# Five stages whose second token tile is transposed two blocks earlier in TensorE's queue

## The chip, the cores and the metric

The kernel runs on one core of one Trainium2 chip. The metric is the time of one execution on the device in microseconds (us). Beside it there is one execution under the hardware profiler; its rows are what this document reads. PE or TensorE is the matmul engine (PEld its weight loads), DVE is VectorE, ACT is ScalarE, POOL is GpSimd, SP is SyncE, which issues the weight DMAs. A difference of under about 0.3%, 2.9 us here, can't be told from no change.

## What is computed

Two small transformer blocks in float32, one after the other, over 256 tokens of width 1024. The first has a differential-attention and Fourier mixer, two gated feed-forward layers and a convolution module; the second a gated linear recurrence and a block attention. What matters here is what stands ahead of five of the large products: a normalised and modulated copy of the state x is multiplied by a weight matrix.

```python
def rmsnorm(x, g):
    x32 = x.astype(jnp.float32)
    y = x32 * lax.rsqrt(jnp.mean(x32 * x32, axis=-1, keepdims=True) + EPS)
    return (y * g.astype(jnp.float32)).astype(x.dtype)

def modulate(h, shift, scale):
    return h * (1 + scale) + shift

def swiglu(h, w1, w3, w2):
    return (jax.nn.silu(h @ w1) * (h @ w3)) @ w2

def conformer_conv(h, pw1_w, ...):
    a, g = jnp.split(h @ pw1_w + pw1_b, 2, axis=-1)
...
        x = x + mod_l[2] * y_l
        x = x + mod_l[5] * swiglu(modulate(rmsnorm(x, ffn_norm_g[i]), mod_l[3], mod_l[4]),
                                  ffn_w1[i], ffn_w3[i], ffn_w2[i])
```

The five products are h @ w1 and h @ w3 of the two feed-forward layers (stages ffn0 and ffn1), the first product of the convolution module (pw1), the input product of the recurrence (rg_in) and the key and value product of the block attention (kv).

## The kernel before

**Products.** Every float32 operand is split into a high and a low part (`hi`, `lo`), and a product is three matmuls: hi by hi, hi by lo, lo by hi (`three`, L2059 to L2063). Each of the three has a 128x128 piece of the state as stationary operand and 512 columns of a weight unit as moving operand. Three such matmuls are called a block here. The 256 tokens are two tiles of 128 (t = 0, 1), the width 1024 is eight pieces of 128 (k = 0 to 7). A weight unit holds four pieces k by 512 columns, so that a chunk of 512 output columns takes two units: j = 0 with k = 0 to 3 and j = 1 with k = 4 to 7. `half(u, j, ..., ts, ks)` (L2068) issues the blocks of unit u for the tiles ts and, of the unit's four pieces, for those in ks. Results of tile t accumulate in PSUM bank t. Units are loaded by SP into `w_land`, copied by ScalarE to `w_hi` and subtracted by VectorE to `w_lo`; three of each exist. A unit counts as used (`s_used`) with the last block of tile 1.

**The first chunk of a stage.** The operand of these five stages isn't ready when the stage before ends, and it is made tile by tile. For one tile: VectorE and ScalarE finish the residual sum and its squares, VectorE the mean, GpSimd the power -1/2 (`rstd`, L518), VectorE scales the tile (`tile_normed`, L1363, output `xn`, semaphore `xn`), TensorE transposes the eight 128x128 pieces into two PSUM banks (`turn_tile`, L2096 to L2101, semaphore `tr`), VectorE applies scale and shift to pieces 0 to 3 (L1400, `xfull` or `kv_full`), ScalarE to pieces 4 to 7 (L755), ScalarE copies each to `xT_hi` (L766), VectorE subtracts it to `xT_lo` (L1383, semaphore `lo`). Each block of a first chunk waits for its own `lo` (L2076).

VectorE does this in the order of `tile_operand` (L1377): the pieces of tile 0, between them a last residual step and the mean of tile 1, then `tile_normed` of tile 1, then at once the first half of the split of the third weight unit (`split_lo_half`, L1370), then the pieces of tile 1, with the unit's second half ahead of the last three subtractions. ScalarE's order is `tile_hi` (L750).

**TensorE's order** is `first_chunk` (L2103): the transposes of tile 0 (in ffn0, ffn1 and kv they have already been issued inside the last half of the stage before, L2427), four blocks of unit u and four of unit u + 1 for tile 0, the transposes of tile 1, then the eight blocks of tile 1. The blocks are numbered b0 to b15 in this document. Each engine runs its instructions in the order in which they are written, and one that waits holds up those behind it.

The transposes of tile 1 go to banks 2 and 3 (AFTER_DENSE) or 3 and 5 (AFTER_FFN), which nothing else reads at that time; the blocks go to banks 0 and 1.

Callers of `first_chunk` are `ffn` (L2485, twice), `dense` (L2407, for pw1 and kv) and the loop of rg_in (L2650). After the first chunk of ffn0 TensorE also waits for the sums of a modulation job (`job_sum`, L1274 on VectorE, summed at L2141) and for a tile of zeros (L596, GpSimd).

Of the kernel before, what the change touches and what calls it, by code (L numbers as in the profile page):

```python
# [182 lines left out]
def build(nc, t_in, out):  # L183
    with ExitStack() as ctx:
        sems = {}

        def sem(name):
            if name not in sems:
                sems[name] = ctx.enter_context(nc.semaphore(name))
            return sems[name]  # L190

        def seen(kind, stage, n):

            return sem(kind), STEPS_BEFORE[kind, stage] + n
# [4 lines left out]
        def place(name, shape, offset, dtype=F32):  # L199
            return nc.alloc_sbuf_tensor_at(name, shape, dtype, offset=ARENA + offset)  # L200
# [8 lines left out]
        xT_hi = place("xT_hi", [P, KT, S], 164 * KB, R32)  # L209
        xT_lo = place("xT_lo", [P, KT, S], 172 * KB, R32)  # L210
# [144 lines left out]
        bank = [ctx.enter_context(nc.psum_tensor(f"bank{i}", [P, 512], F32)) for i in range(8)]  # L355
# [1702 lines left out]
        def _(pe):  # L2058
            def three(dst, hi, lo, whi, wlo, start, stop):  # L2059

                pe.matmul(dst, hi, whi, start=start, stop=False)  # L2061
                pe.matmul(dst, hi, wlo, start=False, stop=False)  # L2062
                return pe.matmul(dst, lo, whi, start=False, stop=stop)  # L2063

            def unit_wait(u, i=None):
                pe.wait_ge(s_lo, at(u + 1, i, 6))

            def half(u, j, hi, lo, banks, last=None, ready=None, ts=range(NT), ks=range(4), part=False):  # L2068

                wh = w_hi[u % N_SPLIT][:, :].rearrange("p (k n) -> p k n", k=4)  # L2070
                wl = w_lo[u % N_SPLIT][:, :].rearrange("p (k n) -> p k n", k=4)
                for t in ts:
                    for k in ks:

                        if ready is not None and ADDS[ready]["lo"] == NT * KT:
                            pe.wait_ge(*seen("lo", ready, KT * t + 4 * j + k + 1))  # L2076
                        elif ready is not None and t == 0:
                            pe.wait_ge(*seen("lo", ready, min(4 * j + k + 1, ADDS[ready]["lo"])))
                        kt = 4 * j + k
                        ins = three(banks[t][:, :], hi[:, kt, t * P:t * P + P], lo[:, kt, t * P:t * P + P],  # L2080
                                    wh[:, k, :], wl[:, k, :], kt == 0, kt == KT - 1)
                    if part and j == 1 and t == 0:
                        ins.then_inc(sem("part"), 1)
                if last is not None:
                    ins.then_inc(last, 1)
                return ins
# [9 lines left out]
            def turn_tile(stage, t, banks):  # L2096

                pe.wait_ge(*seen("xn", stage, t + 1))
                for k in range(KT):
                    pe.transpose(bank[banks[t][k // 4]][:, P * (k % 4):P * (k % 4) + P],  # L2100
                                 xn[:, t, k * P:k * P + P], ident[:, :]).then_inc(sem("tr"), 1)  # L2101

            def first_chunk(stage, u, banks, turned=False):  # L2103

                if not turned:
                    turn_tile(stage, 0, banks)
                for j in range(2):
                    unit_wait(u + j)
                    half(u + j, j, xT_hi, xT_lo, bank[0:2], None, stage, (0,))
                turn_tile(stage, 1, banks)  # L2110
                for j in range(2):
                    half(u + j, j, xT_hi, xT_lo, bank[0:2], s_used, stage, (1,))

# [132 lines left out]
            for c in (2, 3):  # L2246
                for side, (event, b) in enumerate(events[c]):
# [3 lines left out]
                    for j in range(2):  # L2251
                        u = 2 * c + j
# [141 lines left out]
            def dense(stage, n_chunks, ready=None, after=None, before=None, parts=True, job=(), turn_banks=None,  # L2394
# [4 lines left out]
                for c in range(n_chunks):  # L2399
# [4 lines left out]
                    if c == 0 and first is not None:  # L2404
                        first(u, banks)
                    elif c == 0 and turn_banks is not None:
                        first_chunk(ready, u, turn_banks, turn_banks == AFTER_DENSE)  # L2407
                    elif c == 0 and ready == "ln":
                        for t in range(NT):
# [38 lines left out]
            def ffn(layer, loops, first_job):  # L2448
# [26 lines left out]
                def turn_hidden(c, i=None):  # L2475
# [7 lines left out]
                    ins.then_inc(sem("h_turn"), 1)  # L2483

                first_chunk(f"n_ffn{layer}", base, AFTER_DENSE, True)  # L2485
                if layer == 0:
                    job_sums(first_job - 1)
# [160 lines left out]
            for c in range(4):  # L2648
                if c == 0:
                    first_chunk("n_rg", BASE["rg_in"], AFTER_FFN)  # L2650
                for j in range(2 if c else 0):
                    u = BASE["rg_in"] + 2 * c + j
                    unit_wait(u)
                    for t in range(NT):
                        half(u, j, xT_hi, xT_lo, bank[2 * (c % 2):2 * (c % 2) + 2], s_used if t == 1 else None,
                             None, (t,))
                        if (c, j, t) == (1, 0, 0):
                            turn_pair("rg_in", rg_tok, rg_free)(0)
                        for g in {(2, 0, 1): (2, 3), (2, 1, 0): (4, 5), (2, 1, 1): (6, 7)}.get((c, j, t), ()):
                            rg_gate_mm(g)  # L2660
                    if (c, j) == (1, 1):
                        job_sums(15)
                if c == 3:
                    unit_wait(BASE["rg_out"])
                    half(BASE["rg_out"], 0, xT_hi, xT_lo, bank[0:2], None, "rg", (0,))
                if c >= 1:
                    turn_pair("rg_in", rg_tok, rg_free)(c)
                if c == 1:
                    job_turn(15)
                    pe.wait_ge(s_cols, cols_upto(15))  # L2670
                    rg_gate_mm(0)
                    rg_gate_mm(1)
# [214 lines left out]
```

## Time and profile before

| | |
|---|---|
| timed runs | 973.63, 975.66, 975.75 us, median 975.66 |
| the profiled execution's own time | 974.42 us |
| its span, first to last instruction | 972.8 us |
| mean granted TensorE clock over the span | 0.986 of full |
| busy: TensorE, VectorE, ScalarE, GpSimd | 93%, 76%, 48%, 14% |
| the five first chunks begin about (us) | ffn0 206, pw1 408, ffn1 523, rg_in 727, kv 821 |
| bytes moved | 229 MB, 236 GB/s in the mean |

Times in rows are microseconds from the start of the span. Busy time of TensorE includes the modelled end of each matmul, so a matmul of 0.39 us starts about 0.23 us after the one before it; distances between starts say more than durations. A wait row says which engine and line waited for which, with the total, the number of waits and the longest.

### The profile page before, as it was taken

To read this page: it belongs to the slowest core of one execution; us is meant where nothing else is said; L and a number is where in the kernel's file an instruction comes from. 1 tells how busy PE (TensorE), PEld (TensorE's weight loads), DVE (VectorE), ACT (ScalarE), POOL (GpSimd) and SP (SyncE) were. 2 spreads that over 40 slices of the span, in tenths; PEclk is the share of its full clock that TensorE was granted. 3 is DMA by queue.
4 is the path that set the end of the run, shared out by engine and by line. 5 is a ranking of instruction groups with operands and counts; after the bars stand their busy time and mean duration, and the time that the engine had idled before them with its cause. 6 is when DMAs were issued, how large, how long until landed. Compare 5 with 4: busy or idle time off the path is not lost.

```text
span 972.8 us, 12490 instructions
## 1 busy us (share of the span) xinstructions
PE 906.0 (93%) x4323; PEld 711.8 (73%) x4323; DVE 739.7 (76%) x1075; ACT 468.6 (48%) x782; POOL 134.8 (14%) x204
## 2 busy tenths in 40 slices
PE   3899999989999999899988999999979998999995
PEld 1687666767888888677566788888867776778874
DVE  1598779888768677779678877678698888876675
ACT  2462258554344443553185444434435876545661
POOL 0011130405001300020003210021001110001000
PEclk9999999999999999999999999999989999999998
DMA  9998653459989889457525798898857446695001
GB/s 332 375 356 287 225 174 124 168 175 340 379 304 304 314 288 316 159 172 260 201 87 164 254 354 320 281 332 299 290 172 250 130 165 204 227 358 193 23 23 43
DMA packets 121094, 229.09 MB, mean 236 GB/s; under 512 B 8650, under 2 KB 64684, under 8 KB 121050
## 3 DMA queue, kind: packets, MB, share of 16 engines
q1 hardware_dynamic: 94656, 141.57, 42.4%
q0 software_dynamic: 24224, 86.32, 25.5%
q10 hardware_dynamic: 2170, 0.64, 0.3%
q8 instruction: 24, 0.39, 0.2%
q14 instruction: 20, 0.16, 0.0%
HBM read 227.43 MB, written 1.08 MB: 235 GB/s over the span
## 4 chain that ended last, share of the span: by engine, by line
PE 68%; DVE 16%; issue 6%; ACT 4%; DMA 4%; POOL 1%; SPq 0%; POOLq 0%; ACTq 0%; DVEq 0%
PE bank L2061 19%; PE bank L2063 18%; PE bank L2062 18%; DVE job_sum L1274 2%; DVE w_lo L1257 2%; DMA a_land<-ada_w_dram 2%; PE bank L2640 1%; DMA x<-x_dram 1%; DVE x L1339 1%; DMA w_land<-ev_w_in_dram 1%; ACT w_hi L696 1%; DVE tmp L1338 1%; DVE w_lo L1370 1%; PE bank L2481 1%; PE bank L2293 1%
## 5 line engine op out<-in xcount | busy, mean ns | idle before, releaser
L2061 PE MATMUL bank<-w_hi,xT_hi 128*128 128x512 f32 x800 | 322.9, 404 | 16.9 <-DVE xT_lo L1383 10.0
L2063 PE MATMUL bank<-w_hi,xT_lo 128*128 128x512 f32 x800 | 313.2, 392 | 0.0
L2062 PE MATMUL bank<-w_lo,xT_hi 128*128 128x512 f32 x800 | 312.8, 391 | 0.0
L1257 DVE TENSOR_TENSOR w_lo<-w_land,w_hi 128x2048 fp32r<-128x2048 f32 x109 | 250.1, 2298 | 79.8 <-ACT w_hi L696 79.6
L696 ACT ACTIVATE w_hi<-w_land 128x2048 fp32r<-128x2048 f32 x109 | 208.2, 1915 | 110.9 <-PE bank L2063 102.2
L2061 PEld LDWEIGHTS bank<-w_hi,xT_hi 128*128 128x128 f32 x800 | 151.0, 189 | 61.8 <-issue 19.4
L2063 PEld LDWEIGHTS bank<-w_hi,xT_lo 128*128 128x128 f32 x800 | 150.7, 188 | 32.7
L1274 DVE SCALAR_TENSOR_TENSOR job_sum<-a_land,silu_c,job_sum 128x1024 f32<-128x1024 f32 x126 | 163.4, 1297 | 11.0 <-DMA a_land<-mod_w_dram 4.4
L2062 PEld LDWEIGHTS bank<-w_lo,xT_hi 128*128 128x128 f32 x800 | 151.1, 189 | 28.2
L2061 PE MATMUL bank<-w_hi,hT_hi 128*128 128x512 f32 x176 | 69.9, 397 | 2.8 <-DVE hT_lo L1688 2.8
L2063 PE MATMUL bank<-w_hi,hT_lo 128*128 128x512 f32 x176 | 68.7, 390 | 0.0
L2062 PE MATMUL bank<-w_lo,hT_hi 128*128 128x512 f32 x176 | 68.5, 389 | 0.0
L526 POOL DMA_DIRECT2D a_land<-ada_w_dram x40 | 29.3, 732 | 226.8 <-DVE job_sum L1274 226.8
L989 ACT ACTIVATE silu_g<-bank 128x256 f32<-128x256 f32 x44 | 14.5, 382 | 76.1 <-PE bank L2063 76.1
L993 ACT ACTIVATE hT_hi<-bank 128x512 fp32r<-128x512 f32 x22 | 13.2, 599 | 68.1 <-PE bank L2481 68.1
L2061 PEld LDWEIGHTS bank<-w_hi,hT_hi 128*128 128x128 f32 x176 | 33.0, 188 | 13.8 <-issue 7.3
L2063 PEld LDWEIGHTS bank<-w_hi,hT_lo 128*128 128x128 f32 x176 | 33.0, 188 | 7.1
L2062 PEld LDWEIGHTS bank<-w_lo,hT_hi 128*128 128x128 f32 x176 | 33.1, 188 | 6.5
L526 POOL DMA_DIRECT2D a_land<-mod_w_dram x24 | 17.2, 717 | 146.4 <-DVE job_sum L1274 140.7
L1370 DVE TENSOR_TENSOR w_lo<-w_land,w_hi 128x1024 fp32r<-128x1024 f32 x30 | 36.3, 1218 | 0.4 <-ACT w_hi L742 0.4
L726 ACT ACTIVATE sq_half<-x 128x512 f32<-128x512 f32 x24 | 15.2, 631 | 42.9 <-DVE x L1339 42.9
L1684 DVE TENSOR_TENSOR hid<-silu_g,bank 128x256 f32<-128x256 f32 x44 | 16.5, 417 | 23.4 <-ACT silu_g L989 23.4
(327 smaller groups left out, 1115.0 us busy)
## 6 DMA issues: line engine op xcount, KB each, us to landing
w_land<-ffn_w_dram SPq DMA_DIRECT2D x132, 512.0 KB, 5.8
a_land<-ada_w_dram POOLq DMA_DIRECT2D x40, 1024.0 KB, 6.1
a_land<-mod_w_dram POOLq DMA_DIRECT2D x24, 1024.0 KB, 5.8
w_land<-od_pw_w_dram SPq DMA_DIRECT2D x24, 512.0 KB, 5.2
w_land<-ev_w_in_dram SPq DMA_DIRECT2D x20, 512.0 KB, 11.6
w_land<-ada_w_dram SPq DMA_DIRECT2D x16, 512.0 KB, 10.6
a_land<-kv_mod_w_dram POOLq DMA_DIRECT2D x8, 1024.0 KB, 6.6
w_land<-rg_w_in_dram SPq DMA_DIRECT2D x16, 512.0 KB, 5.2
```

The costliest lines, as they stand in the source:

```text
L526: pool.dma_start(a_land[j % 2][:, :].rearrange("p (k n) -> p k n", k=2), kview(w)[:, 2 * j:2 * j + 2, bass.ds(col, D)]).then_inc(a_landed[ ...
L696: act.activation(w_hi[u % N_SPLIT][:, :], w_land[n % N_LAND][:, :], ACT.Copy).then_inc(s_hi, 1)
L726: act.activation(sq_half[:, n % 2, :], x[:, t, 512 * c:512 * c + 512], ACT.Square, accum_out=ss[:, 2 * t + c:2 * t + c + 1]).then_inc(sem( ...
L989: act.activation(silu_g[:, t, :], bank[t][:, 0:256], ACT.Silu).then_inc(sem("silu_g"), 1)
L993: act.activation(hT_hi[:, :, :].rearrange("p k s -> p (k s)"), bank[6][:, :], ACT.Copy).then_inc(sem("hT_hi"), 1)
L1257: dve.tensor_tensor(w_lo[u % N_SPLIT][:, :], w_land[n % N_LAND][:, :], w_hi[u % N_SPLIT][:, :].bitcast(F32), ALU.subtract).then_inc(s_lo, 1)
L1274: ins = dve.scalar_tensor_tensor(out=job_sum[:, :], in0=w, scalar=silu_c[:, c, n:n + 1], in1=job_sum[:, :], op0=ALU.mult, op1=ALU.add)
L1370: return dve.tensor_tensor(w_lo[u % N_SPLIT][:, cols], w_land[n % N_LAND][:, cols], w_hi[u % N_SPLIT][:, cols].bitcast(F32), ALU.subtract)
L1684: dve.tensor_tensor(hid[:, t, :], silu_g[:, t, :], bank[t][:, 256:512], ALU.mult).then_inc(sem("hid"), 1)
L2061: pe.matmul(dst, hi, whi, start=start, stop=False)
L2062: pe.matmul(dst, hi, wlo, start=False, stop=False)
L2063: return pe.matmul(dst, lo, whi, start=False, stop=stop)
```

## The change

In `first_chunk` the call of `half` for tile 0 issues for j = 0 the pieces 0 to 3 as before, but for j = 1 only pieces 0 and 1. Then tile 1 is transposed, and then the two blocks that were left (pieces 2 and 3 of unit u + 1, b6 and b7) are issued. After that tile 1's blocks run as before. All blocks accumulate into the same banks in the same order of k. `turn_tile` begins with a wait for `xn`, which moves with it. No other engine's program is changed.

```diff
                 for j in range(2):
                     unit_wait(u + j)
-                    half(u + j, j, xT_hi, xT_lo, bank[0:2], None, stage, (0,))
+                    half(u + j, j, xT_hi, xT_lo, bank[0:2], None, stage, (0,), range(4 - 2 * j))
                 turn_tile(stage, 1, banks)
+                half(u + 1, 1, xT_hi, xT_lo, bank[0:2], None, stage, (0,), (2, 3))
                 for j in range(2):
                     half(u + j, j, xT_hi, xT_lo, bank[0:2], s_used, stage, (1,))
```

## Rows read from the trace of the kernel before

**Rows 1.** The page, first part: busy time, share and instructions of each engine.

```profile
PE 906.0 (93%) x4323; PEld 711.8 (73%) x4323; DVE 739.7 (76%) x1075; ACT 468.6 (48%) x782; POOL 134.8 (14%) x204
```

**Rows 2.** Waits, whole span: who waited for whom, total us, times, longest us.

```profile
PE bank L2061 <- DVE xT_lo L1383: 10.0, 19, 1.3
...
PE bank L2100 <- DVE xn L1363: 8.1, 4, 3.6
```

**Rows 3.** Timeline of ffn0: start us, us, engine, line, operation [idle before <-releaser].

```profile
201.68 0.75 DVE L1363 TENSOR_SCALAR xn<-x,rstd 128x1024 f32<-128x1024 f32 x1 [0.69 <-POOL rstd L518]
...
202.49 1.09 PE L2100 MATMUL bank<-ident,xn 128*128 128x128 f32 x8 [1.63 <-DVE xn L1363]
...
203.34 0.47 PE L2061 MATMUL bank<-w_hi,xT_hi 128*128 128x512 f32 x1
...
204.11 0.40 PE L2061 MATMUL bank<-w_hi,xT_hi 128*128 128x512 f32 x1
...
210.33 0.75 DVE L1363 TENSOR_SCALAR xn<-x,rstd 128x1024 f32<-128x1024 f32 x1
...
211.00 1.22 DVE L1370 TENSOR_TENSOR w_lo<-w_land,w_hi 128x1024 fp32r<-128x1024 f32 x1
211.00 0.40 PE L2061 MATMUL bank<-w_hi,xT_hi 128*128 128x512 f32 x1
...
212.39 1.04 PE L2100 MATMUL bank<-ident,xn 128*128 128x128 f32 x8
213.03 0.73 DVE L1400 TENSOR_SCALAR xfull<-bank,a_col,mcol 128x128 f32<-128x128 f32 x2 [0.82 <-PE bank L2100]
...
214.17 0.50 PE L2061 MATMUL bank<-w_hi,xT_hi 128*128 128x512 f32 x1 [0.73 <-DVE xT_lo L1383]
...
214.96 0.39 PE L2061 MATMUL bank<-w_hi,xT_hi 128*128 128x512 f32 x1
...
217.69 0.50 PE L2061 MATMUL bank<-w_hi,xT_hi 128*128 128x512 f32 x1
...
218.49 0.39 PE L2061 MATMUL bank<-w_hi,xT_hi 128*128 128x512 f32 x1
```

**Rows 4.** Timelines of pw1, ffn1, rg_in and kv: scaling of tile 1, and b8.

```profile
412.30 0.75 DVE L1363 TENSOR_SCALAR xn<-x,rstd 128x1024 f32<-128x1024 f32 x1
...
416.13 0.50 PE L2061 MATMUL bank<-w_hi,xT_hi 128*128 128x512 f32 x1 [0.73 <-DVE xT_lo L1383]
...
527.89 0.53 POOL L596 MEMSET zeros<- 128x512 bf16 x1
...
527.98 0.98 DVE L1363 TENSOR_SCALAR xn<-x,rstd 128x1024 f32<-128x1024 f32 x1
...
531.81 0.50 PE L2061 MATMUL bank<-w_hi,xT_hi 128*128 128x512 f32 x1 [0.74 <-DVE xT_lo L1383]
...
733.21 0.75 DVE L1363 TENSOR_SCALAR xn<-x,rstd 128x1024 f32<-128x1024 f32 x1
...
733.60 0.40 PE L2061 MATMUL bank<-w_hi,xT_hi 128*128 128x512 f32 x1
...
736.76 0.50 PE L2061 MATMUL bank<-w_hi,xT_hi 128*128 128x512 f32 x1 [0.73 <-DVE xT_lo L1383]
...
825.67 0.75 DVE L1363 TENSOR_SCALAR xn<-x,rstd 128x1024 f32<-128x1024 f32 x1
...
829.51 0.50 PE L2061 MATMUL bank<-w_hi,xT_hi 128*128 128x512 f32 x1 [0.73 <-DVE xT_lo L1383]
```

**Rows 5.** The chain that ended last, behind ffn0's first chunk: start us, us, what.

```profile
221.58 0.55 POOL zeros L596
```

**Rows 6.** Stretches: length, busy PE, PEld, DVE, ACT, POOL; PEclk, DMA share, GB/s.

```profile
194.40:218.70 24.30, 20.63 (x94) 15.66 (x93) 20.36 (x43) 14.16 (x37) 2.06 (x3) 1.00 0.52 174
...
243.00:267.30 24.30, 24.30 (x116) 19.59 (x116) 19.06 (x15) 9.37 (x9) 2.15 (x3) 1.00 1.05 378
...
724.20:731.00 6.80, 5.98 (x18) 4.74 (x19) 5.71 (x14) 4.35 (x17) 0.00 (x0) 0.50 0.50 154
```

## The prediction

> **What bounds the kernel now.** I read the page's busy shares first: TensorE is busy 906.0 of 972.8 us [rows 1]. Then who waited for whom: on TensorE the waits that touch this change are for the turned operand and for the normalised tile [rows 2]. Then the timeline of one of the five stages, ffn0 [rows 3], the same steps in the other four [rows 4], the chain behind the first [rows 5], and the busy time in slices [rows 6], which tells whether time won early in a stage is still there at its end.
>
> I call three matmuls of 128x512 (the call of `three`) a block. A stage's first chunk has sixteen: b0 to b7 for token tile 0, b8 to b15 for tile 1. The kernel before runs b0 to b7, eight transposes of tile 1, then b8 to b15. Rows 3 show what is wrong with that. The last transposes start at 212.39, VectorE gets its first turned piece at 213.03 (it had sat idle), and b8 starts at 214.17, after TensorE sat idle 0.73 us waiting for `xT_lo`. VectorE's scaling of tile 1 had ended long before, at 210.33 + 0.75 = 211.08. So between two stretches of work lies a dead time: transposes, scale, split, subtract, one after the other with nothing else to run. In rows 4 the four other stages have the same picture.
>
> **The change, part by part.** Nothing is added or removed: the same 48 matmuls and 8 transposes per stage. The transposes and their one wait (for the scaled tile, semaphore `xn`) move ahead of b6 and b7. No DMA is issued by the moved step, and SP's and GpSimd's queues are not passed. Behind the wait on TensorE's queue stand, newly, b6 and b7, which are ready by then; nobody waits for their results until tile 1 is done (the count for a used weight unit goes up only at tile 1's blocks), so delaying them costs nothing on another engine.
>
> The new start T of the transposes is the later of b6's old start and the scaled tile. In ffn0 b6 started at 211.00 and the tile is ready at 211.08. The first turn of the same kind started 0.06 after its scale ended (202.43 to 202.49) [rows 3]. So T = scale's end + 0.06, in ffn0 211.14, a new wait of 0.14. In rg_in it is the longest: 733.21 + 0.75 + 0.06 = 734.02 against b6 at 733.60, so 0.42 [rows 4].
>
> From T: eight transposes take the queue 0.85 (202.49 to 203.34), the block after them 0.77 (203.34 to 204.11) [rows 3]. A block in a running stream takes a little under 0.70; from the distance of b6 to the turn, (212.39 - 211.00) / 2, it is 0.69. So b8 can start at T + 0.85 + 0.77 + 0.69 = T + 2.31, if its operand is there.
>
> Operand side: VectorE runs the half split `w_lo` (1.22) right behind the scale, from 211.00, and can then take the turned piece at about 212.15 instead of 213.03 [rows 3]; the transposes of T = 211.14 give their first four by 211.78 (0.64 from turn to piece, as 212.39 to 213.03). From the piece to b8 it took 214.17 - 213.03 = 1.14, so b8's operand is there at about 213.29; TensorE gets there at 213.45. Both hang on the scale's end, so the margin of some 0.16 is the same in all five stages. The next late thing is TensorE itself, no longer the operand.
>
> Gains at b8, old start less (scale's end + 0.06 + 2.31) [rows 3, 4]:
> ffn0: 214.17 - 213.45 = 0.72
> pw1: 416.13 - (412.30 + 0.75 + 2.37) = 0.71
> ffn1: 531.81 - (527.98 + 0.98 + 2.37) = 0.48
> rg_in: 736.76 - (733.21 + 0.75 + 2.37) = 0.43
> kv: 829.51 - (825.67 + 0.75 + 2.37) = 0.72
> Sum 3.06 us.
>
> In ffn1 the scale took 0.98 where it takes 0.75 elsewhere, and GpSimd's memset of `zeros` runs at that moment (527.89 for 0.53) [rows 4]. In the old order these 0.23 us were hidden, in the new they are on TensorE's path, and they are in the sum. The Trainium skill, page Advanced Engine Details and Errata, section DVE Details, says that one of VectorE's two ports is shared with GpSimd; that is a rule against this change, since it makes TensorE wait for an operation that GpSimd can stretch, and the trace agrees in this one stage.
>
> Second term: a block that starts after a wait takes 0.79 (b8 to b9, 214.17 to 214.96), and so does b13 (217.69 to 218.49), which waited for its operand behind the second half split [rows 3]. In a stream it is 0.69. b8 no longer waits: 5 x 0.10 = 0.50. For b13: its operand came 217.69 - 213.03 = 4.66 after the first piece, now at 212.15 + 4.66 = 216.81; TensorE gets there at 213.45 + 5 x 0.69 = 216.90. That is 0.09 ahead, which may be too little to load weights in advance, so this second restart costs between nothing and what it costs now: a gain of 0 to 0.50, I take the middle, 0.25.
>
> The bound on moving the transposes between b5 and b6 of one accumulation: I know of no row for a turn inside tile 0's own blocks, but the previous dense stage has the same form (202.49 to 204.11 lies inside its last half) and that is the price used. Below nothing it cannot be, since the same eight transposes run anyway; above, the whole 0.85 + 0.08 is already counted.
>
> Sum: 3.06 + 0.50 + 0.25 = 3.8 us, bounds 3.55 and 4.05.
>
> **Does it last to the end?** In ffn0 the old chain behind b15 is not TensorE's but VectorE's: last subtractions, two `job_sum` steps, `zeros` by GpSimd at 221.58, then the next block [rows 5]. VectorE was idle before 213.03 and moves forward by 213.03 - 212.15 = 0.88, so this chain moves as much as the 0.82 to 0.92 that TensorE gains. After it TensorE is busy 24.30 of 24.30 us in the slice from 243, the first of twelve such slices in the two feed-forward loops [rows 6], so time won is kept. In pw1, rg_in and kv what follows waits for the chunk's last matmul or for VectorE, both earlier. I see nothing with its own clock there. All 3.8 us should reach the end.
>
> Against the profiled execution: 974.42 - 3.8 = 970.6. The three timed runs are at 973.63 to 975.75 with a median 1.2 above the profiled one; the mean of all four is 974.87, and I set the forecast from that: 971.1.
>
> **Rivals.**
> (A) Weight supply takes the place of the wait. In the slice from 243 us the DMA share is 1.05, at 378 GB/s [rows 6]: if the stream is the true limit of the feed-forward loops, TensorE, arriving earlier, waits for weights there and the gains of ffn0 and ffn1 (0.9 and 0.6) are lost; what is left is 3.8 - 1.5 = 2.3, so 972.6. Against it: TensorE has no idle in that slice, and the slice is the fullest one. Together with any other loss of one or two stages' gain (972 to 974): 20%.
> (B) The change does nothing: the dead time is VectorE's and ScalarE's own and only moves. It would need VectorE to be late at b8 by itself. The half split after the scale is the candidate; with it I get 213.29 against 214.17, so this cannot hide more than 0.16 of the gain unless the split waits too. Time 974.9. 6%.
> (C) Slower: the scaled tile is late. In the old order it had 212.39 - 211.08 = 1.31 us to spare; now it has less than nothing (0.08 to 0.36 late already). A tile later by d costs TensorE d at once, in each stage, with b6 and b7 stuck behind it although ready. The gain at the end of tile 1 is 0.6 to 0.9 per stage, so the change turns into a loss when the tile comes on average 0.76 us later than in this trace, and a loss of 0.3% needs about 1.35. With 1.35 in each of five stages: 974.9 - 3.8 + 6.75 = 977.8. For it: the stretch of 0.23 in ffn1. Against it: nothing that the scale depends on is changed. 4%.
> (D) Clock. Granted clock was half (1.2 of 2.4 GHz, 0.50 in the row) from 724.2 to 731 us, after TensorE had idled up to 3.6 us waiting for the tile ahead of rg_in [rows 2, 6]. New waits are 0.42 at most, so I expect no new such stretch; but if one of 6.8 us fell into a saturated loop it would lose half of it, 3.4 us: 974.5. The Trainium skill, page TensorE: Matmul & The Clock Gate, section Part 4: PE-mode transpose, says that transposes do not count as busy time for the gate; by that rule eight of them where matmuls ran could bring such a stretch, and the time would be those 974.5. The row speaks against it for this pattern: the granted clock is 1.00 in the slice from 194 to 219, with both turns of ffn0 in it. 5%.
> (E) More than I count: the removal of idle time keeps a stretch at full clock that was at half, or the runs fall low; 968 to 969.5. 5%.
>
> **How the numbers follow.** Forecast 60%, A 20%, B 6%, C 4%, D 5%, E 5%. A measurement of this kernel can tell about 0.3%, 2.9 us, from no change. Faster by more than that: the forecast, E, and a part of A: 0.69. Within: most of A, B, D and the low edge of the forecast: 0.26. Slower: C and the tail of D: 0.05. The range: the forecast with its bounds and the spread of executions (about 1 us either way) is 969.8 to 972.4; A and part of D reach to 974.5. From 969.0 to 974.6 leaves out B, C, most of E.
>
> **What would show it.** In the profile of the changed kernel, in each of five stages: transposes of tile 1 between the sixth and seventh block, starting 0.06 after the scale; b8 2.3 us after them with no wait for `xT_lo`; VectorE idle before the turned piece of tile 1 gone (it was 0.8); TensorE's total wait for `xT_lo` down from 10.0 by about 3.6 and a new wait for `xn` of 0.1 to 0.4 five times, 1.2 in all. The half split of unit 2 and the last subtractions come 0.6 to 0.9 earlier. If b8 still waits, step "operand side" is wrong; if b8 is early and the span is not, the step "does it last" is; the point where the two timelines' difference shrinks will say which rival it is.

## The result, and the profile after

The changed kernel takes 970.59 us (median of its executions beside 975.80 of the kernel before, six each). The ratio is 0.9922 with an interval of 0.9896 to 0.9949. One execution of the changed kernel took 2325.56 us and is left out as a slow one; why isn't known, and the other five lie from 968.63 to 971.68. Forecast was 971.1, range 969.0 to 974.6; carried to the 975.66 given before, the ratio makes 968.05, below the range. So the change gained, at first sight, 7.6 us where the sum says 3.8. The two medians by themselves differ by 5.2 us only. The ratio stands for a kernel before at 970.59 / 0.9922 = 978.2 us; of its six executions three are the ones on record ahead of the prediction (median 975.66), and the other three are 975.84, 978.41 and 979.68 (median 978.41), so the ratio looks like one to these three. A second comparison, with more executions (below), gave 0.995 with 0.9932 to 0.9968, some 4.9 us. What follows has two questions: is the sum of 3.8 right, and where does the rest come from?

The profiled execution took 970.08 us, with a span of 968.4 against 972.8 before. First the page of the changed kernel: span, busy time and the granted clock in slices (the share of full speed that TensorE was given, in tenths).

```profile
span 968.4 us, 12490 instructions
...
PE 906.3 (94%) x4323; PEld 713.0 (74%) x4323; DVE 740.0 (76%) x1075; ACT 468.5 (48%) x782; POOL 136.9 (14%) x204
...
PEclk9999999999999999989999999999989999999998
```

TensorE has the same busy time and count as in [rows 1]; what went is idle time. The waits over the whole span, who waited for whom (total us, times, longest):

```profile
PE bank L2100 <- DVE xn L1363: 8.0, 6, 3.6
...
PE bank L2061 <- DVE xT_lo L1383: 6.5, 14, 1.3
```

Against [rows 2] the wait for `xT_lo` has five cases and 3.5 us less, and the wait for `xn` two cases more. The timeline of ffn0 shows the mechanism (start us, us, engine, line, operation):

```profile
199.39 0.75 DVE L1363 TENSOR_SCALAR xn<-x,rstd 128x1024 f32<-128x1024 f32 x1 [0.69 <-POOL rstd L518]
...
208.04 0.75 DVE L1363 TENSOR_SCALAR xn<-x,rstd 128x1024 f32<-128x1024 f32 x1
208.71 1.22 DVE L1370 TENSOR_TENSOR w_lo<-w_land,w_hi 128x1024 fp32r<-128x1024 f32 x1
208.85 1.09 PE L2100 MATMUL bank<-ident,xn 128*128 128x128 f32 x8
209.69 0.48 PE L2061 MATMUL bank<-w_hi,xT_hi 128*128 128x512 f32 x1
209.84 0.73 DVE L1400 TENSOR_SCALAR xfull<-bank,a_col,mcol 128x128 f32<-128x128 f32 x2
211.18 0.40 PE L2061 MATMUL bank<-w_hi,xT_hi 128*128 128x512 f32 x1
...
214.62 0.39 PE L2061 MATMUL bank<-w_hi,xT_hi 128*128 128x512 f32 x1
...
216.01 0.39 PE L2061 MATMUL bank<-w_hi,xT_hi 128*128 128x512 f32 x1
```

The tile is scaled at 208.04 + 0.75 = 208.79, the turn starts 0.06 later at 208.85, b8 at 211.18 (2.33 after the turn) with no wait, b13 at 214.62 with none, b15 at 216.01. VectorE takes the turned piece right behind the half split, without the idle 0.82 of [rows 3]. Everything ahead of the scaling is untouched by the change, so I measure in each stage from the start of tile 0's scaling (here 199.39; before 201.68, [rows 3]). The last block of the kernel before:

```profile
219.19 0.39 PE L2061 MATMUL bank<-w_hi,xT_hi 128*128 128x512 f32 x1
```

b15 went from 219.19 - 201.68 = 17.51 to 216.01 - 199.39 = 16.62 (rows are rounded, so such a difference is good to 0.02). The other four stages, pw1, ffn1, rg_in and kv, of the changed kernel: the scaling of tile 1, then b8.

```profile
409.10 0.75 DVE L1363 TENSOR_SCALAR xn<-x,rstd 128x1024 f32<-128x1024 f32 x1
...
412.24 0.40 PE L2061 MATMUL bank<-w_hi,xT_hi 128*128 128x512 f32 x1
...
525.64 0.98 DVE L1363 TENSOR_SCALAR xn<-x,rstd 128x1024 f32<-128x1024 f32 x1
...
529.00 0.40 PE L2061 MATMUL bank<-w_hi,xT_hi 128*128 128x512 f32 x1
...
730.35 0.76 DVE L1363 TENSOR_SCALAR xn<-x,rstd 128x1024 f32<-128x1024 f32 x1
...
733.48 0.40 PE L2061 MATMUL bank<-w_hi,xT_hi 128*128 128x512 f32 x1
...
822.22 0.75 DVE L1363 TENSOR_SCALAR xn<-x,rstd 128x1024 f32<-128x1024 f32 x1
...
825.35 0.40 PE L2061 MATMUL bank<-w_hi,xT_hi 128*128 128x512 f32 x1
```

None of these b8 waits, where all of [rows 4] waited 0.73 or 0.74. The table is the ruler for all that follows: the start of b15 after the start of tile 0's scaling, in us, read the same way from each kernel's timeline. The gain is the sum of the five differences to the first line. The kernels whose names begin with e_ are the experiments of the next section.

| kernel | ffn0 | pw1 | ffn1 | rg_in | kv | gain |
|---|---|---|---|---|---|---|
| before | 17.50 | 16.54 | 17.49 | 17.96 | 17.51 | |
| before, again (e_none) | 17.50 | 16.55 | 17.51 | 17.97 | 17.51 | -0.04 |
| the change | 16.62 | 15.64 | 16.79 | 17.38 | 16.59 | 3.98 |
| the change, again (e_two) | 16.58 | 15.66 | 16.80 | 17.37 | 16.58 | 4.01 |
| e_one | 16.81 | 15.88 | 16.82 | 17.36 | 16.79 | 3.34 |
| e_three | 17.23 | (17.28) | 17.44 | 17.98 | 17.21 | 0.60 |
| e_late_old | 17.76 | 16.82 | 17.78 | 18.05 | 17.76 | -1.17 |
| e_late_new | 18.01 | 17.07 | 18.01 | 18.30 | 18.01 | -2.40 |
| e_split3 | 15.74 | (16.01) | 15.92 | 17.39 | 15.71 | 5.70 |
| e_split5 | 15.71 | 15.48 | 16.03 | 17.60 | 15.71 | 6.47 |
| e_memset | 16.59 | 15.65 | 16.60 | 17.36 | 16.60 | 4.20 |
| e_split3m | 15.73 | 15.64 | 15.71 | 17.35 | 15.70 | 6.87 |

A value in brackets fell into a stretch at half clock and isn't in the sum. In rg_in every kernel has such a stretch, before and after the change alike, over some 7 us from the start of tile 0's scaling and done before b5; these values are kept. (In e_three the sum of the other four stands against 3.08 for the change in the same four. In e_split3, whose pw1 is the changed kernel's own, that stage's 0.90 comes to it: 6.6.) The two executions of one kernel, twice, agree within 0.05 in every stage on this ruler; their spans don't.

### The profile page after: what moved, and what is told of

Read it like the earlier page. It is cut to its first block, busy times and chain, and to the rows that moved or that the text cites. A ratio compares the mean times of both kernels' runs of the same rounds, so it can differ in the third digit from the quotient of the medians.

```text
span 968.4 us, 12490 instructions
## 1 busy us (share of the span) xinstructions
PE 906.3 (94%) x4323; PEld 713.0 (74%) x4323; DVE 740.0 (76%) x1075; ACT 468.5 (48%) x782; POOL 136.9 (14%) x204
## 4 chain that ended last, share of the span: by engine, by line
PE 67%; DVE 16%; issue 6%; ACT 5%; DMA 4%; POOL 1%; SPq 0%; POOLq 0%; ACTq 0%; DVEq 0%
PE bank L2061 19%; PE bank L2063 18%; PE bank L2062 18%; DVE job_sum L1274 2%; DVE w_lo L1257 2%; PE bank L2641 1%; DMA a_land<-ada_w_dram 1%; DMA x<-x_dram 1%; DVE x L1339 1%; DVE w_lo L1370 1%; DMA w_land<-ev_w_in_dram 1%; ACT w_hi L696 1%; DVE tmp L1338 1%; PE bank L2482 1%; PE bank L2142 1%
```

## The experiments

Time is judged in two ways: by the ratio to the kernel before, run beside it, and by the ruler. Beside them stands a third figure, the clock-free one. It is an estimate from 161 timed executions: 72 of the kernel before, in three comparisons, and 89 of the nine kernels timed beside it more than once. A straight line of the time against the mean granted clock of each execution is laid through them, with a constant for each kernel. It says 0.54 us (0.07 either way) more for each 0.001 of mean clock less, and for each kernel a difference to the one before that is free of the clock's share. Its 95% interval stands behind it in brackets.

**The comparison itself.** The kernel before against itself, and the changed kernel again, beside 32 executions of the kernel before (median 977.53, from 973.94 to 980.91).

> The kernel before, unchanged, timed against itself. Theory 1 (the change is worth 3.8 us by the order of the queue alone, and what the first comparison showed beyond that, some 7.6 us, is the draw of stretches at half clock): ratio 1.000, but single runs spread over 5 us or more, and the profile shows the half-clock stretches at other places than the first profile of before did, with VectorE's timeline moving by 1 to 3 us at each. Theory 2 (the change itself avoids stretches at half clock): single runs of before all share the same stretches, so they agree within 2 us.

> The changed kernel, two blocks ahead, once more. Theory 1: ratio about 0.996 (3.8 of 975), and wherever the profile's timeline jumps other than in the five first chunks there is a stretch at half clock in one of the two profiles. In the five chunks VectorE's timeline moves forward by 0.9, 0.9, 0.55, 0.6 and 0.9 us. Theory 2: ratio again about 0.992.

Measured: e_none 976.59, ratio 0.9997 (0.998 to 1.0015). e_two 972.81, ratio 0.995 (0.9932 to 0.9968). With the clock taken out: -0.1 (0.8 either way) and -4.0 (0.9 either way). Mean clock of the executions 0.9795 for the kernel before, 0.9813 for e_two, 0.9809 for e_none: the change has no more clock than the kernel before has against itself. So the change is worth about 4 us here, and the reading that it also avoids half-clock time finds no support. The single executions of e_none spread over 4.6 us, where that reading wanted 2. What the spans do instead shows in one row: ffn0's first scaling, ahead of which no instruction differs. First e_none, then e_two:

```profile
199.41 0.75 DVE L1363 TENSOR_SCALAR xn<-x,rstd 128x1024 f32<-128x1024 f32 x1 [0.69 <-POOL rstd L518]
```

```profile
205.07 0.75 DVE L1363 TENSOR_SCALAR xn<-x,rstd 128x1024 f32<-128x1024 f32 x1 [0.69 <-POOL rstd L518]
```

From 199.4 to 205.1: 5.7 us apart in work that is the same. The kernel before had 201.68, the changed one 199.39. The clock is part of it. Stretches of e_two ahead of that row (length, busy PE, PEld, DVE, ACT, POOL, then granted clock, DMA share, GB/s):

```profile
20.00:26.90 6.90, 3.65 (x16) 3.27 (x16) 4.32 (x10) 3.16 (x6) 0.71 (x1) 0.51 1.09 352
43.90:47.30 3.40, 3.40 (x10) 2.63 (x9) 3.26 (x12) 2.03 (x5) 0.00 (x0) 0.50 1.06 385
119.00:125.80 6.80, 6.40 (x25) 4.44 (x25) 2.77 (x6) 0.58 (x2) 1.44 (x2) 0.50 0.69 246
```

That is 17.1 us at 1.2 GHz; e_none has only the first of them, 6.9. The 10.2 us more go with 5.7 us more time; by the line above they would cost 2.8 (10.2 us at half clock are 0.0052 of the mean), so about half of it is not explained. The Trainium skill, page TensorE: Matmul & The Clock Gate, section Part 1: The HAM clock gate, says of a kernel's start that the number of matmuls at the low clock varies from run to run of one kernel. The rows agree in kind, and show such stretches at 43.9 and 119 us as well, far from the start.

**How far ahead.** One block and three blocks instead of two.

```diff
-half(u + j, j, xT_hi, xT_lo, bank[0:2], None, stage, (0,), range(4 - 2 * j))
+half(u + j, j, xT_hi, xT_lo, bank[0:2], None, stage, (0,), range(4 - j))
-half(u + 1, 1, xT_hi, xT_lo, bank[0:2], None, stage, (0,), (2, 3))
+half(u + 1, 1, xT_hi, xT_lo, bank[0:2], None, stage, (0,), (3,))
```

(for three: `range(4 - 3 * j)` and `(1, 2, 3)`)

> Tile 1 turned one block ahead (b7 alone behind the turn). By the sum: the transposes start at b7's old start, after the scaled tile is ready, so no new wait; the operand is then the last thing at b8 in ffn0, pw1 and kv. b8 comes earlier than before by 0.69, 0.68, 0.66, 0.60, 0.68 = 3.3 us, and b8 still pays the 0.10 of a restart. Gain at the stages' ends about 3.3 to 3.6, so 0.2 to 0.5 less than two blocks ahead; in ffn1 and rg_in a little more than two ahead at b8. The rival, that waiting for the scaled tile costs much in the two-block form, would make one block ahead the faster by 1 us or more.

> Tile 1 turned three blocks ahead (b5, b6, b7 behind the turn). By the sum the transposes can't start before the scaled tile is there, so they start when they do two blocks ahead, and three blocks instead of two come after them: b8 0.69 later in each stage, 5 x 0.69 = 3.45 us lost against two ahead, a gain over before of only 0.3. VectorE's timeline in the chunks moves as two ahead, since the operand is made as early. The rival, that VectorE's and ScalarE's chain sets the end and TensorE has time to spare, expects three ahead to be as fast as two.

Measured: e_one 974.17, ratio 0.9964 (0.9944 to 0.9983), ruler 3.34, clock-free -3.4 (0.8). e_three 975.87, ratio 0.9986 (0.9969 to 1.0003), ruler 0.60, clock-free -1.3 (0.8). e_one lies inside the 3.3 to 3.6 that the fixed start of the turn gives. e_three was to gain 0.3 in five stages and gained 0.60 in four: an early turn cost 0.62 a stage and not 0.69. By the clock-free figures alone e_one can't be told from the changed kernel (-3.4 and -4.0); that it is the worse rests on the ruler. The timelines say why. In e_one the operand is late again at b8, by a little (the turn starts only at 213.04, of a tile whose scaling ended at 212.45), and in e_three the turn waits with three blocks stuck behind it. First e_one (turn, then b8 with the 0.50 of a restart), then e_three:

```profile
213.04 1.04 PE L2100 MATMUL bank<-ident,xn 128*128 128x128 f32 x8
...
214.82 0.50 PE L2061 MATMUL bank<-w_hi,xT_hi 128*128 128x512 f32 x1
```

```profile
212.15 1.09 PE L2100 MATMUL bank<-ident,xn 128*128 128x128 f32 x8 [0.66 <-DVE xn L1363]
...
215.16 0.39 PE L2061 MATMUL bank<-w_hi,xT_hi 128*128 128x512 f32 x1
```

Where the tile is late, one block ahead is as good as two (rg_in 17.36 and 17.37, ffn1 16.82 and 16.80); in the three others two wins by 0.2. Of the four places tried, none to three blocks ahead, the best is where the turn meets the scaled tile.

**What a late tile costs.** In `tile_operand` the half split of the next weights is put in front of the scaling of tile 1, in the kernel before and in the changed one.

```diff
                     if n == KT:
                         low(n - 1)
-                        tile_normed(stage, 1)
                         split_lo_half(unit, 0, half_ready(unit))
+                        tile_normed(stage, 1)
```

> The kernel before, with two neighbours on VectorE exchanged in the five first chunks: the half weight split (1.22 us) now runs ahead of the scaling of tile 1, so the scaled tile is there 1.2 us later and nothing else is. Rival C of the prediction said that the old order had 1.31 us to spare in ffn0. By that: no loss in ffn0, pw1 and kv, 0.2 to 0.3 in ffn1 and rg_in, 0.4 to 0.5 us in all, ratio 1.000. If instead the scaled tile was already what set the old order's end, it costs 5 x 1.2 = 6 us.

> The changed kernel (two blocks ahead) with the same exchange on VectorE, so the scaled tile is 1.2 us later. By rival C's price (a tile later by d costs TensorE d at once, b6 and b7 stuck behind the wait): 5 x 1.2 = 6 us against the changed kernel, so slower than the kernel before by some 2.3 us, ratio 1.002; last blocks of the chunk 1.2 later in each stage than two ahead. If the wait were cheap because VectorE's chain sets the end, only some 0.3 per stage would be lost, since VectorE does the same work in the same total.

Measured, beside 23 executions of the kernel before (978.55): e_late_old 979.75, ratio 1.0019 (0.9999 to 1.0039), ruler -1.17, clock-free +1.6 (0.9). e_late_new 980.61, ratio 1.002 (1.0004 to 1.0036), ruler -2.40, clock-free +3.3 (0.9), that is 6.4 us behind the changed kernel by the ruler and 7.3 by the clock-free figure. ffn0 of e_late_old, then of e_late_new:

```profile
211.12 1.23 DVE L1370 TENSOR_TENSOR w_lo<-w_land,w_hi 128x1024 fp32r<-128x1024 f32 x1 [0.39 <-ACT w_hi L742]
212.27 0.75 DVE L1363 TENSOR_SCALAR xn<-x,rstd 128x1024 f32<-128x1024 f32 x1
213.07 1.09 PE L2100 MATMUL bank<-ident,xn 128*128 128x128 f32 x8
214.90 0.50 PE L2061 MATMUL bank<-w_hi,xT_hi 128*128 128x512 f32 x1 [0.74 <-DVE xT_lo L1383]
```

```profile
212.79 0.75 DVE L1363 TENSOR_SCALAR xn<-x,rstd 128x1024 f32<-128x1024 f32 x1
213.59 1.09 PE L2100 MATMUL bank<-ident,xn 128*128 128x128 f32 x8 [1.43 <-DVE xn L1363]
214.43 0.47 PE L2061 MATMUL bank<-w_hi,xT_hi 128*128 128x512 f32 x1
...
215.90 0.40 PE L2061 MATMUL bank<-w_hi,xT_hi 128*128 128x512 f32 x1
```

The old order lost more than the 0.4 to 0.5 us expected: 1.17. The exchange makes the scaling 1.46 us later in ffn0 (10.11 after the first one instead of 8.65), more than the 1.22 of the split, since the split itself waits 0.39 for ScalarE, and that is also more than the 1.31 to spare. The old order absorbs most of it: its turn starts 10.91 - 10.71 = 0.20 later and b15 0.26. The new order has nothing to absorb it with: the turn starts 1.45 later (10.91 instead of 9.46), with a wait of 1.43, and b15 1.39. With the late tile the new order is slower than the old, 18.01 against 17.76 in ffn0. This is rival C, with its price: a tile later by d costs the new order d. Averaged over the five stages a delay of 3.98 / 5 = 0.80 us eats the gain (I had said 0.76).

**Making the tile earlier.** If the scaled tile now sets the pace, the next gain lies in front of it. VectorE's queue there holds the second half split of the previous weight unit, ahead of the first turned piece of tile 0. e_split3 moves it in ffn0, ffn1 and kv to the middle of tile 0's eight pieces, behind the last residual step and the subtraction of the fourth piece; e_split5 does it in all five stages, and puts GpSimd's `zero_ffn` of ffn1 one DMA later.

```diff
                     if k >= 1:
                         low(n - 1)
+                    if n == 4 and stage in LATE_SPLIT:
+                        split_lo_half(unit - 1, 1, (s_hi, unit)).then_inc(s_lo, 1)
...
                 if unit < UNITS:
                     split_lo_half(unit, 0, half_ready(unit))
-                    split_lo_half(unit, 1, (s_hi, unit + 1)).then_inc(s_lo, 1)
```

> The changed kernel, and in ffn0, ffn1 and kv the second half split of the stage's second weight unit (1.13 to 1.22 us on VectorE), which stood between the scaling of tile 0 and its first turned piece, is moved behind the last residual step, where VectorE sat idle 0.79 us. By the same way of summing: first turned piece 1.1 us earlier, b0 1.0 earlier (TensorE is then busy until it), the scaled tile 1 about 0.8 earlier, and since TensorE's end follows the scaled tile, 0.8 x 3 = 2.4 us beyond the changed kernel: 6.2 against before, ratio 0.9936. If the scaled tile doesn't set the end, the gain stays at 3.8, ratio 0.996.

> As the one before, in all five stages, and GpSimd's memset of the zeros in ffn1 moved behind its next DMA issue, so that it no longer runs beside the scaling of tile 1. In pw1 and rg_in the piece comes 0.3 to 0.5 earlier but little slack follows: 0.1 to 0.2 each. The scaling in ffn1 takes 0.75 instead of 0.98 if the memset stretched it: 0.23 more. In all 6.6 to 6.9 against before, ratio 0.993. If the memset has nothing to do with it, the scaling stays at 0.98.

Measured: e_split3 970.51, ratio 0.993 (0.991 to 0.9951), clock-free -6.5 (1.1). e_split5 972.9, ratio 0.9941 (0.9921 to 0.9961), clock-free -5.0 (1.1). By the ruler 6.6 and 6.5. ffn0 of e_split3: the split, now at 208.02, the scaling, the turn, b15:

```profile
208.02 1.22 DVE L1370 TENSOR_TENSOR w_lo<-w_land,w_hi 128x1024 fp32r<-128x1024 f32 x1
...
210.38 0.75 DVE L1363 TENSOR_SCALAR xn<-x,rstd 128x1024 f32<-128x1024 f32 x1
211.18 1.09 PE L2103 MATMUL bank<-ident,xn 128*128 128x128 f32 x8
...
218.35 0.40 PE L2064 MATMUL bank<-w_hi,xT_hi 128*128 128x512 f32 x1
```

Its scaling comes 7.77 after the first one (8.65 before), and b15 at 15.74: the 0.88 by which the tile is earlier is the 0.88 by which b15 is. Widening this to pw1 gave 0.16 there and cost 0.22 in rg_in, where the tile became later (9.66 after the first instead of 9.41), so five stages are no better than three. For e_split5 the two figures part: 6.47 by the ruler, 5.0 (1.1) by the clock-free one of six executions. What the missing 1.5 us are was not found; between the chunks its profile has the distances of before (ffn0 to pw1 185.43, rg_in to kv 75.24, kv to the end 138.20) wherever no stretch at half clock lies.

**The stretched scaling of ffn1.** The forecast had put its 0.98 us (0.75 elsewhere) down to GpSimd's memset of `zeros` beside it. e_split5 seemed to speak against that: the memset issued one DMA later, and the scaling took 1.06. Its timeline shows that the two still met, and that the memset too took 1.03 where it takes 0.53:

```profile
529.70 1.06 DVE L1363 TENSOR_SCALAR xn<-x,rstd 128x1024 f32<-128x1024 f32 x1
```

```profile
530.19 1.03 POOL L596 MEMSET zeros<- 128x512 bf16 x1
```

So two more kernels: the memset moved behind a row load and three bias loads, in the changed kernel (a single, profiled execution) and in e_split3 (beside 17 executions of the kernel before, 979.46).

```diff
             pow_tiles("n_ffn1")
-            zero_ffn()
             load_row("final_g", bias_gate, "final_g_in")
...
             load_bias(17, mod_b[1:2, 2 * D:3 * D])
+            zero_ffn()
```

> The changed kernel with GpSimd's memset of `zeros` in front of ffn1 moved behind the bias loads, some 6 us later, into a time when VectorE is idle. If the memset is what stretched ffn1's scaling of tile 1 from 0.75 to 0.98 us, the scaling is 0.75 and the last block of ffn1's first chunk starts 16.56 us after the start of tile 0's scaling instead of 16.79. If the stretch is ffn1's own (where the tiles lie in memory, or the DMA issues beside it), the scaling stays 0.98 and the last block at 16.79. The 0.23 us can't be seen in the time of one run, whose spread is some 7 us.

> The later split in three stages and the memset moved, both. By the positions in the traces: 6.6 us under the kernel before as in the version with the later split alone, and 0.23 more, so 6.8 us, ratio 0.993. By the reading that the split's version only fell on a lucky chip or hour (its second half of gain not real): 3.8 to 4, ratio 0.996. In the trace the last block of ffn1's first chunk starts 15.69 us after the start of tile 0's scaling if the memset was the cause, 15.92 if not.

Measured: e_memset has its scaling at 0.75 and b15 at 16.60 instead of 16.79. e_split3m 971.84, ratio 0.9934 (0.9912 to 0.9956), clock-free -6.6 (0.8), ruler 6.87 for an expected 6.8. ffn1 of e_memset, VectorE's scaling, then the memset, now 6.8 us after the scaling starts:

```profile
526.33 0.75 DVE L1363 TENSOR_SCALAR xn<-x,rstd 128x1024 f32<-128x1024 f32 x1
```

```profile
533.09 0.54 POOL L596 MEMSET zeros<- 128x512 bf16 x1
```

The memset is the cause. The other reading of e_split3, that the second half of its gain was a lucky chip, falls as well: in a third comparison, on another chip, e_split3m is again 6.6 us ahead. The 0.2 us of the memset can't be seen in its time. e_split3 and e_split3m beat both kernels: 2.5 us ahead of the changed one by the clock-free figures, 2.6 to 2.9 by the ruler. They were never timed beside the changed kernel, only each beside the kernel before, and the 2.5 has an interval of some 1.3 either way.

## Why the prediction was right and wrong

**Mechanism, right.** Removed waits, new waits and order came as written. The new waits for `xn` were, by the distance from b5's end to the turn, 0.14, 0.12, 0.35, 0.42 and 0.12, together 1.15 (predicted 1.2); the wait for `xT_lo` fell by 3.5 (predicted 3.6).

**The sum at b8, right.** T, the start of tile 1's turn, is the scaling's end plus 0.06; T to b8 was 2.32 or 2.33 (2.31). Gains at b8: 0.70, 0.70, 0.48, 0.41, 0.71, together 3.00 (3.06).

**The restarts, slightly low.** From b8 to b15 the gain was 0.98 where 0.75 was set down: b13 in ffn0 doesn't wait any more and pays no restart, so nearly the whole of the term bounded by 0 and 0.50 came, not its middle. Total 3.98 for 3.8, inside 3.55 to 4.05.

**"Does it last", right.** From b15 of one stage to the scaling of the next: ffn0 to pw1 185.41 before and 185.39 after, rg_in to kv 75.26 and 75.27, from kv's b15 to the end 138.21 and 138.21. No weights were waited for in the feed-forward loops; rival A is out, and B with it.

**The clock, half right.** ffn1 to rg_in took 186.98 and 187.13, pw1 to ffn1 98.21 and 99.96. In the second there is a half-clock stretch that came in the profile of after, behind pw1. The same window of before, then of after:

```profile
420.60:427.40 6.80, 6.80 (x43) 4.77 (x42) 3.57 (x4) 4.17 (x7) 1.60 (x3) 1.00 0.89 306
```

```profile
420.60:427.40 6.80, 6.80 (x20) 5.22 (x17) 4.19 (x4) 4.40 (x5) 4.77 (x4) 0.50 0.55 199
```

That looks like rival D, but e_none has a stretch there too (at 423.8), and e_memset, with the change in it, has none and takes 96.80. So it comes and goes without regard to the change. The kernel before, with none there either, takes 98.21; what these two differ in is a later stretch of 3.4 us, at 485.2 in before and at 495.8 in e_memset, and e_three, with its own at 486.3, takes 98.41. So the 1.75 us between the two profiles are about 3.15 for the new stretch less 1.4 that go with the other place of the later one. What TensorE did in after before the clock fell at 420.6: no idle, but narrow matmuls of 31 rows, of which these are the last sixteen:

```profile
419.74 1.20 PE L2541 MATMUL bank<-taps,tap_waves 31*32 31x256 f32 x16
```

In all five profiles with a stretch between 420 and 433 us (e_none, after, e_two, e_late_old, e_split3) it begins 0.1 to 1.3 us after the start of the last of these. The other profiles run the same matmuls and keep the full clock there, so these matmuls alone don't bring it about.

The chunk of ffn0, with the transposes now among the matmuls, kept its clock:

```profile
199.40:216.50 17.10, 15.00 (x70) 11.36 (x70) 15.52 (x36) 10.90 (x30) 1.49 (x2) 1.00 0.50 166
```

The other chunks have no new stretch (rg_in's first 7 us are at half clock in both profiles). The rule of the Trainium skill on transposes, which rival D took up, changed nothing here.

**GpSimd's port, right.** The 0.23 us in ffn1 belong to the memset, as e_memset shows. By the Trainium skill, page Advanced Engine Details and Errata, section Mode Summary, the second port of VectorE is shared with GpSimd, and GpSimd's instructions and VectorE's two-port ones block each other. The trace agrees that the two disturb each other, for the scaling (a TENSOR_SCALAR); no row says which ports it uses. It shows the price as 0.23 to 0.31 us for a memset that takes 0.53 alone, less than a wait for its end: in the kernel before the memset had 0.44 us left when the scaling began, and the scaling lost 0.23.

**What failed: the reference and its spread.** The forecast is a sum, 974.87 less 3.8, and the term that was mis-sized is the first, with its width. Both the 974.87 and "the spread of executions (about 1 us either way)" were read off four executions of the kernel before. Seventy-two of them, in three comparisons, reach from 973.07 to 981.07, with medians of 977.5, 978.6 and 979.5 where I had 974.9. The forecast of 971.1 is near the 970.59 measured, and that is partly luck: the same change gave 972.81 in the second comparison. The lower bound of 969.0 took in only the mechanism's own bounds and not the comparison's: against a kernel before at 978.2 the same 970.59 is a ratio of 0.9922, and this, carried to 975.66, is 968.05. That value lies in rival E (968 to 969.5, given 5%), by its second half, that the runs fall low; for its first half, that idle time taken out keeps a stretch at full clock, e_two and e_none show nothing. The profiles of before and after differ by 4.37 us of span, and this is made of -2.29 ahead of the first changed instruction, -3.98 in the five chunks, +1.75 from pw1 to ffn1 and +0.15 elsewhere: the two profiles would have looked right for a wrong reason had I read only the total.

**What stays open.** In the first comparison the ratio 0.9922 has an interval (0.9896 to 0.9949) that just meets that of the second (0.9932 to 0.9968). In the two traces of the changed kernel 3.98 and 4.01 us are shown. Part of the rest of the first comparison is the clock: its five executions of the changed kernel have a mean granted clock of 0.984 where e_two's nine have 0.981, which by the line above is some 1.6 us. Put into that line, the five lie 5.2 us (1.2) below the kernel before at equal clock, e_two 4.0 (0.9); the 1.2 between them is inside the intervals. This takes the kernel before from the other comparisons, since the clocks of its executions beside the five are not listed. So some 2 us of the 7.6 are left to a few executions drawn from a spread of 8 us, the simplest reading, and it was not tested.

## What to carry to other kernels

When a step stands behind a producer with work in front of it, move it forward until it just meets the producer and no further: one block too late cost 0.13 us a stage (3.98 less 3.34, over five), one block too early 0.6 (3.08 less 0.60, over four), and from there each us by which the producer is later is nearly an us of the kernel (1.39 for 1.46 in ffn0). Then look at what stands in front of the producer on its own queue; here that was worth another 2.6 us. Size the range by the spread of the kernel against itself, and compare positions relative to the last point that the change can't touch, which agreed within 0.05 us where spans differed by 5.

## What the runs showed of the hardware

Two executions of the same instructions differed by 5.7 us in their first 205 us (e_none and e_two), and 10.2 us more at 1.2 GHz went with it. Over 161 executions 0.001 less mean granted clock goes with 0.54 us more time. The stretches at half clock do not keep their places: between 407 and 433 us six of the twelve profiles have one and six have none; the kernel before has one in one of its two profiles and none in the other. And an overlap of GpSimd's memset with VectorE's scaling slowed both when the scaling had started first (memset 0.53 to 1.03, scaling 0.75 to 1.06), and only the scaling (to 0.98) when the memset had.
